# Rows of a head exchanged by copies of 32 rows on VectorE and ScalarE in place of a matrix product, and the first half of x loaded first

## What is computed

```python
def apply_rope(x, cos, sin):
    x1, x2 = jnp.split(x.astype(jnp.float32), 2, axis=-1)
    ...
    return jnp.concatenate([x1 * c - x2 * s, x2 * c + x1 * s], axis=-1).astype(x.dtype)
```

## Time and profile before

| what | value |
|---|---|
| median of 3 runs | 2049.03 us (2048.91 to 2052.25) |
| the profiled execution | 2048.79 us, its span 2047.0 us |
| TensorE | busy 1982.0 us, 97% of the span |
| VectorE | busy 1062.2 us, 52% |
| ScalarE | busy 967.0 us, 47% |
| GpSimd | busy 755.9 us, 37% |
| granted TensorE clock, mean | 0.992 of full speed |

### The profile page before, as it was taken

The page is one execution under the profiler, slowest core; times in us unless marked ns, Lnnn a source line. Parts: engine busy times, 40 slices in busy tenths (PEclk is TensorE's granted clock), DMA queues, the critical chain, the costliest instruction groups (busy, mean ns, idle before and its releaser), DMA issues.

```text
span 2047.0 us, 25966 instructions
## 1 busy us (share of the span) xinstructions
PE 1982.0 (97%) x10216; PEld 1646.8 (80%) x10216; DVE 1062.2 (52%) x1935; ACT 967.0 (47%) x1700; POOL 755.9 (37%) x341
## 2 busy tenths in 40 slices
PE   6999999999999999999999999999999999999997
PEld 6778888877778877777788888888878888888886
DVE  3365544267665667777647464312536584444214
ACT  4355534256653465555536444422555464444323
POOL 2422233433324333333343444444242324444442
PEclk9999999999999999999999999999999999999999
DMA  4311122311113222222222232333221213232332
GB/s 174 93 42 44 51 73 82 93 52 45 56 35 99 78 82 64 77 77 73 73 83 83 96 106 93 101 91 96 75 58 41 73 62 113 93 102 94 95 93 70
DMA packets 50058, 162.60 MB, mean 79 GB/s; under 512 B 5392, under 2 KB 12176, under 8 KB 49808
## 3 DMA queue, kind: packets, MB, share of 16 engines
q1 hardware_dynamic: 49504, 159.54, 24.6%
q10 hardware_dynamic: 432, 1.40, 0.2%
HBM read 158.82 MB, written 2.10 MB: 79 GB/s over the span
## 4 chain that ended last, share of the span: by engine, by line
PE 84%; DVE 11%; ACT 3%; issue 2%; DMA 0%; POOL 0%; SPq 0%; ACTq 0%; DVEq 0%
PE ps L1809 20%; PE ps L1812 20%; PE ps L1810 20%; PE ps L1859 4%; PE ps L1874 3%; PE ps L1821 2%; PE ps L1822 2%; PE ps L1824 2%; PE ps L1843 2%; PE ps L1867 2%; DVE tmp L2374 1%; DVE s_xbc L2353 1%; PE ps L1836 1%; PE ps L1834 1%; PE ps L1837 1%
## 5 line engine op out<-in xcount | busy, mean ns | idle before, releaser
L2549 POOL TENSOR_TENSOR wl<-st,wh 128x1024 fp32r<-128x1024 f32 (+2 forms) x311 | 721.8, 2323 | 1206.2 <-ACT wh L1981 1206.0
L1809 PE MATMUL ps<-xh,wh 128*128 128x512 f32 x1368 | 559.1, 409 | 0.0
L1981 ACT ACTIVATE wh<-st 128x1024 fp32r<-128x1024 f32 (+2 forms) x311 | 313.9, 1010 | 517.1 <-PE ps L1812 450.5
L1812 PE MATMUL ps<-xh,wl 128*128 128x512 f32 x1368 | 534.3, 391 | 0.0
L1810 PE MATMUL ps<-xl,wh 128*128 128x512 f32 x1368 | 533.1, 390 | 0.0
L1809 PEld LDWEIGHTS ps<-xh,wh 128*128 128x128 f32 x1368 | 257.2, 188 | 57.7 <-issue 10.9
L1812 PEld LDWEIGHTS ps<-xh,wl 128*128 128x128 f32 x1368 | 256.7, 188 | 55.8 <-POOL wl L2549 0.8
L1810 PEld LDWEIGHTS ps<-xl,wh 128*128 128x128 f32 x1368 | 257.5, 188 | 52.4 <-issue 5.3
L2508 DVE SCALAR_TENSOR_TENSOR tmp<-ps,vec,tmp 128x510 f32<-128x510 f32 (+1 forms) x176 | 131.3, 749 | 222.6 <-ACT tmp L2160 219.6
L2466 DVE SCALAR_TENSOR_TENSOR res<-res,ps 128x512 f32<-128x512 f32 (+1 forms) x37 | 22.7, 614 | 211.0 <-PE ps L1812 203.3
L1809 PE MATMUL ps<-fa_h,wh 128*128 128x512 f32 x308 | 120.6, 392 | 0.0
(11 more groups left out here) (280 smaller groups left out, 3554.1 us busy)
## 6 DMA issues: line engine op xcount, KB each, us to landing
st<-in_f_up SPq DMA_DIRECT2D x88, 512.0 KB, 3.2
st<-in_s_xbc SPq DMA_DIRECT2D x32, 512.0 KB, 3.5
st<-in_f_dn SPq DMA_DIRECT2D x32, 512.0 KB, 3.5
st<-in_o_fm SPq DMA_DIRECT2D x24, 512.0 KB, 3.5
st<-in_e_fm SPq DMA_DIRECT2D x21, 512.0 KB, 3.6
st<-in_s_z SPq DMA_DIRECT2D x16, 512.0 KB, 3.5
st<-in_s_out SPq DMA_DIRECT2D x16, 512.0 KB, 3.6
st<-in_f_dn SPq DMA_DIRECT2D x16, 384.0 KB, 3.1
```

The lines of the kernel that those rows point to most:

```text
L1809: e.matmul(u.bank.ap, hi, x.h[:, kk, :], start=first, stop=False)
L1812: e.matmul(u.bank.ap, lo, x.h[:, kk, :], start=False, stop=last).then_inc(S["mm"], 1)
L1981: e.activation(P.mem["wh"][w.m % NWR][:, 0:w.n], P.mem["stage"][w.m % NSTAGE][:, 0:w.n], ACT.Copy).then_inc(S["w_hi"], 1)
L2549: e.tensor_tensor(P.mem["wl"][w.m % NWR][:, 0:w.n], P.mem["stage"][w.m % NSTAGE][:, 0:w.n], P.mem["wh"][w.m % NWR][:, 0:w.n].bitcast(F32), ...
```

## The change

The rotation no longer uses PE: four copies, each of 32 rows and 512 columns, write g's rows in exchanged order into a tile in SBUF, each on ScalarE or on VectorE, whichever the planner's clock has free first; the product with the sine table then reads that tile. The constants are laid out anew, with the tables behind the rest, and are loaded in two parts. The first half of x no longer shares the DMA engines with the tables and the broadcast row, which come behind all of x; the second and third weights wait for the first half of x to land. The first table load of ScalarE waits for nothing. `first_norm` adds the 8 squared blocks on VectorE and sums the result with one product for each half. Small steps that need the broadcast row or the vectors are put later. The planner's times of DMAs are changed.

```diff
-    "pe": ("mm", "mm_half", "mm_tok", "ones", "blk", "perm", "score", ...
+    "pe": ("mm", "mm_half", "mm_tok", "ones", "blk", "score", ...
...
-LENGTH = {"pe": 440, "act": 620, "dve": 692, "pool": 1280, "sp": 3500, "actq": 3500}
+LENGTH = {"pe": 440, "act": 620, "dve": 692, "pool": 1280, "sp": 1300, "actq": 1300}
...
+           "y_d": 746, "gnrm": 746, "swap_a": 620, "swap_d": 390, ...
...
-PE_DEEP, HOP, OVERLAP = 165, 36, 90
+PE_DEEP, DMA_DEEP, HOP, OVERLAP = 165, 2200, 36, 90
...
-        over = [self.w[m - NSTAGE].hi, self.w[m - NSTAGE].lo] if m >= NSTAGE else []
+        over = [self.w[m - NSTAGE].hi, self.w[m - NSTAGE].lo] if m >= NSTAGE else self.xload[0] if m else []
...
     def rope_g(self, g):
         x = yield from self.taken(self.tmp)
         dst = yield from self.taken(self.tmp)
-        rp = yield from self.taken(self.aux)
-        t = yield ("perm", rp, g, g.ready)
         b2 = yield ("rope_c", dst, g, g.ready, self.rope_ready)
-        b1 = yield ("rope_s", x, rp, t, self.rope_ready)
-        rp.release(b1)
+        t = []
+        for b in range(4):
+            on = "swap_a" if self.idle["act"] + 230 < self.idle["dve"] else "swap_d"
+            rows, other = slice(32 * b, 32 * b + 32), slice(32 * (b ^ 1), 32 * (b ^ 1) + 32)
+            t.append((yield (on, x.ap[other, :], g.ap[rows, :], g.ready, x.freed)))
+        b1 = yield ("rope_s", x, t, self.rope_ready)
         b3 = yield ("rope_add", dst, x, b1, b2)
         x.release(b3)
-        g.release(t, b2)
+        g.release(b2, *t)
...
-    P.put("table", "natural_log_exp_and_others", P.pload)
+    P.put("table", "natural_log_exp_and_others", [])
...
     def first_norm(i):
         cs = HALF[i]
-        bank = yield from P.taken(P.aux)
+        ss = []
         for k in range(8):
             s = yield from P.taken(P.tmp)
-            q = yield ("sq", s.ap[:, cs], s.freed, res[:, k, cs], P.xload[i][k], 256)
-            t = yield ("ones", bank.ap[:, cs], bank.freed, s.ap[:, cs], [q, P.pload], k == 0, k == 7, 256)
-            s.release(t)
+            s.ready = [(yield ("sq", s.ap[:, cs], s.freed, res[:, k, cs], P.xload[i][k], 256))]
+            ss.append(s)
+            for s in ss[k - 2:k - 1] if k < 7 else ss[5:8]:
+                if s is not ss[0]:
+                    t = yield ("acc", ss[0].ap[:, cs], s.ap[:, cs], ss[0].ready, s.ready, 256)
+                    ss[0].ready = [t]
+                    s.release(t)
+        acc = ss[0]
+        bank = yield from P.taken(P.aux)
+        t = yield ("ones", bank.ap[:, cs], bank.freed, acc.ap[:, cs], [t, P.pload], True, True, 256)
+        acc.release(t)
...
-    P.pload = [P.put("const_in"), P.put("vec_in"), P.put("bro_in")]
+    P.pload = [P.put("const_in"), P.put("vec_in")]
...
+    P.later = [P.put("bro_in"), P.put("table_in")]
+    P.rope_ready = P.later
...
-    e.dma_start(P.mem["const"], P.T["const"]).then_inc(S["const_in"], 16)
+    e.dma_start(P.mem["const"][:, 0:C_COS], P.T["const"][:, 0:C_COS]).then_inc(S["const_in"], 16)
...
+        elif kind == "swap_a":
...
+            e.activation(dst, src, ACT.Copy).then_inc(S["swap_a"], 1)
...
+        elif kind == "swap_d":
...
+            e.tensor_copy(dst, src).then_inc(S["swap_d"], 1)
         elif kind == "rope_s":
-            x, rp, permuted, table = o
-            dve.wait_ge(permuted)
+            x, swapped, table = o
+            dve.wait_ge(swapped)
             dve.wait_ge(table)
-            dve.freed(x)
-            e.tensor_tensor(x.ap, rp.ap, P.c(C_SIN, 512), ALU.mult).then_inc(S["rope_s"], 1)
+            e.tensor_tensor(x.ap, x.ap, P.c(C_SIN, 512), ALU.mult).then_inc(S["rope_s"], 1)
...
+        elif kind == "table_in":
+            e.dma_start(mem["const"][:, C_COS:C_N], T["const"][:, C_COS:C_N]).then_inc(S["table_in"], 16)
```

More of the change, by code:

```diff
@@ L21 @@
 NWR = 3
[L23 to L32, removed]
+C_ID, C_ONE, C_BLK, C_PERM, C_TRI, C_CAUS = 0, 128, 256, 384, 512, 640
+C_INV, C_E6, C_E5, C_SGN, C_E5S, C_L20 = range(768, 774)
+C_SEL, C_COS, C_SIN = 774, 808, 1320
+C_N = 1832
 V_SIZES = [("ev_norm", 8), ("a_qn", 1), ("a_kn", 1), ("b_qn", 1), ("b_kn", 1), ("od_norm", 8),
@@ L70 @@
             "dt_e", "dt_ln", "a_exp", "ct_hi", "sel", "wend_e", "gsq", "gln", "grs", "msq", "ln_out", "ln_hi", "csq",
-            "f0", "fsilu", "sine", "lat", "q_in", "v_a", "head_hi", "gate_in", "gate_s"),
-    "dve": ("nrm", "split_lo", "v_in", "va_out", "bias_s", "bias_m", "neg_sink", "neg_g", "qk_n", "rope_s", "rope_add",
+            "f0", "fsilu", "sine", "lat", "q_in", "v_a", "head_hi", "swap_a", "gate_in", "gate_s"),
+    "dve": ("nrm", "split_lo", "v_in", "va_out", "bias_s", "bias_m", "neg_sink", "neg_g", "qk_n", "swap_d", "rope_s", "rope_add",
             "mask", "add_b", "mn", "sink_mn", "flip_d", "sink_x", "sums", "rec", "o_n", "y_g", "res_add", "acc",
@@ L78 @@
     "pool": ("w_lo", "rope_c"),
-    "sp": ("w_in0", "w_in1", "w_in2", "x_in0", "x_in1", "x_in2", "x_in3", "bias_in", "lqk_in", "pos_in", "out"),
-    "actq": ("const_in", "vec_in", "bro_in"),
+    "sp": ("w_in0", "w_in1", "w_in2", "x_in0", "x_in1", "x_in2", "x_in3", "bro_in", "table_in", "bias_in", "lqk_in",
+           "pos_in", "out"),
+    "actq": ("const_in", "vec_in"),
 }
@@ L201, in __init__ @@
         self.nsplit = self.nload = 0
-        self.idle = {n: 0.0 for n in STEPS}
+        self.idle = {n: 0.0 for n in STEPS} | {"sp": 1200.0, "actq": 700.0}
         self.ends = {}
@@ L267, in put @@
         self.idle[name] = t - (OVERLAP if name in ("act", "dve") else 0)
-        self.ends[step] = t + (PE_DEEP if name == "pe" else 0)
+        self.ends[step] = t + (PE_DEEP if name == "pe" else DMA_DEEP if kind in DMA else 0)
         return step
@@ L920, in even_layer @@
     tb, tv = [], []
-    tneg = P.put("neg_sink", P.B("sink", 0, 8), P.pload)
-    tgain = [P.put("neg_g", P.V(n), P.pload) for n in ("a_qn", "b_qn")]
+    tneg, tgain = [], []
     qs, ks = ring(mem["qz"]), ring(mem["kz"])
@@ L928, in bias @@
     def bias():
+        for n in ("a_qn", "b_qn"):
+            tgain.append((yield ("neg_g", P.V(n), P.pload)))
         for h in range(8):
@@ L931, in bias @@
             tb.append((yield ("bias_m", bt[0:64, h, 192:256], t)))
+            if h == 0:
+                tneg.append((yield ("neg_sink", P.B("sink", 0, 8), P.later)))
     def prep(fb, j, gain, rope, key, pool):
         u = yield from P.proj_g(x, [w[j]])
-        while None in gates.t[0:4]:
-            yield lambda: None not in gates.t[0:4]
+        while None in gates.t[0:4] or len(tgain) < 2:
+            yield lambda: None not in gates.t[0:4] and len(tgain) == 2
         P.start(4, P.qk_prep_g(u, (P.V(gain), tgain), rope, key, pool,
@@ L1848, in pe_program @@
             e.matmul(st.ap, P.c(C_BLK), s.ap, start=True, stop=True).then_inc(S["blk"], 1)
[L1849 to L1852, removed]
-            e.matmul(rp.ap, P.c(C_PERM), g.ap, start=True, stop=True).then_inc(S["perm"], 1)
         elif kind == "score":
@@ L2178, in act_program @@
             e.activation(hi, src, ACT.Copy, scale=scale).then_inc(S["head_hi"], 1)
+        elif kind == "swap_a":
+            dst, src, ready, freed = o
+            act.wait_ge(ready)
+            act.wait_ge(freed)
+            e.activation(dst, src, ACT.Copy).then_inc(S["swap_a"], 1)
         elif kind == "q_in":
@@ L2235, in dve_program @@
             e.scalar_tensor_tensor(dst.ap, u.bank.ap, gain, r.ap, ALU.mult, ALU.mult).then_inc(S["qk_n"], 1)
+        elif kind == "swap_d":
+            dst, src, ready, freed = o
+            dve.wait_ge(ready)
+            dve.wait_ge(freed)
+            e.tensor_copy(dst, src).then_inc(S["swap_d"], 1)
         elif kind == "rope_s":
-            x, rp, permuted, table = o
-            dve.wait_ge(permuted)
+            x, swapped, table = o
+            dve.wait_ge(swapped)
             dve.wait_ge(table)
-            dve.freed(x)
-            e.tensor_tensor(x.ap, rp.ap, P.c(C_SIN, 512), ALU.mult).then_inc(S["rope_s"], 1)
+            e.tensor_tensor(x.ap, x.ap, P.c(C_SIN, 512), ALU.mult).then_inc(S["rope_s"], 1)
         elif kind == "rope_add":
@@ L2421, in dve_program @@
             dve.wait_ge(ready)
-            dve.wait_ge(P.pload)
+            dve.wait_ge(P.later)
             dve.freed(s0)
```

16 lines of the change are left out of this document (8 added, 8 removed).

## The result

The changed kernel takes 2061.78 us (median of 4 runs, 2058.55 to 2065.17) against 2048.97 before (4 runs): a ratio of 1.006, 95% interval 1.0043 to 1.0077. It is slower by 12.8 us, where 2026 was forecast. The profiled execution took 2062.17 us with a span of 2060.4.

What follows compares the result with a forecast made beforehand. The prediction took TensorE, busy 97% of the span, as the bound; 2048.79 - 7.4 (start) - 15.4 (rotation) = 2026.0 us. Its forecast was 2018 to 2033 (54%), its wider range 2014 to 2038.

Steps and rivals of the forecast that it cites:

- Rotation: -22.4 + 7.0 = -15.4 us: All 26 rotations: 22.4 us of products leave TensorE, 7.0 come back as waits; bounds -22.4 and -5.
- the 7.0 given back: TensorE's new waits from rotations: 4.3 us for ten in the odd layer, 2.7 for the other sixteen.
- The rival that ended on this side: Slower: every copy and sine product stands behind a whole GpSimd subtraction, 9.2 us a rotation; about +27, 2076 us; 5%.
- The products' 22.4 us: Rotation: 26 products of 0.86 us each, taken off TensorE as the bound engine.
- VectorE's price: Each rotation costs VectorE 1.3 us of copies, 1.3 behind the cosine product and 0.6 of holds: 3.2 us more.
- The rule made of it: Odd layer, 450 to 600 us: VectorE's demand (136) equals TensorE's (136.3), so half of 8.6 us returns as waits, 4.3.
- Forecast -4.3 + 0.9 for the five rotations of each: Rotations outside the odd layer's two stretches: products of 0.86 us each removed, a fifth taken back as waits.
- Forecast -7.4: Start: first projection 6.9 us earlier, sums 3.0 less, a new wait of 2.5; bounds -11.9 and -4.
- One addition: 9.9: Start, first norm: after the last square at 9.4 us, one VectorE addition of 0.43 us ends at 9.9.
- the loads: Start: the two landings of x's first half come 1.8 us earlier, at 6.6 and 8.1 us.
- The new wait of 2.5 us between the halves: Start: TensorE finishes the first half at 27.5 us, the second is ready at 30; a 2.5 us wait.
- the sums' 3.0 us: Start, behind the first projection: 14 TensorE sums of 0.215 us move to VectorE, saving 3.0 us.

Runs made afterwards that it cites:

- rot_only: The kernel before with only the rotation changed to copies, its start as before: 2072.07 us, ratio 1.0099.
- no_exchange: rot_only without the copies, the sine product reading g itself, so neither product nor copies run: 2040.01 us, ratio 0.9944 to the kernel before.
- copies_beside: The kernel before, its product kept, with each rotation's four copies also run into a tile that nobody reads: 2079.65 us, ratio 1.0135.
- beside_true: copies_beside with the planner told 806 ns for a VectorE copy, 960 for sine product and add: 2064.6 us, ratio 1.0073 to the kernel before.
- start_only: The changed kernel with the old rotation by the product: 2044.94 us, ratio 0.9975 to the kernel before.
- cos_after: rot_only with GpSimd's cosine product given after the copies and waiting for them: 2066.61 us, ratio 1.0084 to the kernel before.
- rot_true: rot_only with the planner told 806 ns for a VectorE copy (was 390), 960 for sine product and add (was 692): 2038.88 us, ratio 0.9943.
- 806 and 960: Planner's ns for a VectorE copy, and for sine product and add: 2038.88 us set in rot_only, 2038.34 in the whole change.
- 700 and 850: Planner's ns for a VectorE copy, and for sine product and add: 2069.14 us set in rot_only, 2061.29 in the whole change.

## Why the prediction was wrong

**The step that failed** is "Rotation: -22.4 + 7.0 = -15.4 us", and in it the 7.0 given back. The rotation's sign was wrong: alone it costs 20 us (rot_only). The rival that ended on this side was put at 5% and made to depend on VectorE needing more than the stretch has; the stretch's work took 125 us of VectorE, less than its 150.

- *The products' 22.4 us.* In the odd layer TensorE's work fell by 11.6 us (332.3 to 320.7) for a forecast of 13.8. But no_exchange shows that only 11.5 of 22.4 come back even without copies. The rest turned into waits and clock, 7.2 us of it in the odd layer.
- *VectorE's price.* Forecast 3.2 us for a rotation; VectorE grew by 76 us, of which the 14 further sums of the start are 8, so 67/26 = 2.6. This was sized about right; the share on VectorE was 67 copies, not 78.
- *The rule made of it.* I took it that waits arise where VectorE's demand nears TensorE's, and gave back 4.3 of 8.6 us. In the odd layer they rose by 16.6 us with VectorE 64% busy. What the waits show is which step stands behind the rotation's: the copies are ready together, up to four go into VectorE's queue in a row, and the softmax's mixing and copies, for which TensorE waits with its own queue in order, stand behind them and behind whatever GpSimd holds. copies_beside shows that this costs 28 us with these planned times and beside_true 15 with others, no step waiting for the copies. A share of busy time can't show that.
- *The clock, left out.* The prediction gave the rotation's new waits no price in clock. Of the odd layer's +14.4 us the clock is +9.4: -11.6 of work, +16.6 of waits, +9.4 of clock.
- *The even layer and the latent attention.* Forecast -4.3 + 0.9 for the five rotations of each, measured +1.6 and +1.0. In the even layer TensorE's work fell by 5.1 us, but its waits went from 6.3 to 12.2 us; the clock took only 0.8 us more. In the latent attention the waits went from 7.6 to 11.6.
- *The start.* Forecast -7.4, measured -4.8 to the first full projection in the change and -7.2 in start_only. "One addition: 9.9" was mis-sized, since three sums follow the last square (10.9 in start_only), and the change's last one was held for some 2.2 us more; so the first projection gained 3.9 us and not 6.9. Of the other terms the loads came near what was worked out, the first square at 5.9 and the fifth at 8.2 us for 6.6 and 8.1, and the hold of the first xl was there. The new wait of 2.5 us between the halves did not come: from 18.72 to 41.1 us the longest wait is 0.2. Nor did the sums' 3.0 us come back in full; this stretch is 0.9 us shorter, for a forecast of 0.5. That the -7.2 of start_only is so near the forecast is in part luck, errors of both signs.
- *Holds.* Rightly foreseen that copies and the sine product would be held, up to 2.6 and 2.7 us. Not foreseen was that the copies push other instructions, down to one of a single column, behind GpSimd. cos_after shows only that a hold moved from the copies to the add gains 3 us by the ratios.

**What is settled and what is not.** Shown: the start gains, the rotation loses; the loss is TensorE's waits and the clock that falls after them, in the odd layer above all; the copies cost even where no step waits for them, and without one on VectorE 12 of the 20 us go; with the planner's times and share changed, the same rotation takes from 2039 to 2072 us. In the table the seven kernels without the product whose VectorE is busy for 227 us or more have the longest waits, 23 to 30 us; the six with 219 to 225 wait 13 to 21. But holds are counted in busy time, so this goes with the waits and is not shown to cause them. The amount of holding does not tell a good order from a bad one: summed over VectorE's instructions of the odd layer, the time above the shortest record of the same line and shape is 32 us before, 52.3 in rot_only and 51.5 in rot_true, with 26.0 and 14.5 us of waits in the last two. Of waits over 1 us for the mixing or its copy, rot_only has seven, six of them close behind a held instruction; rot_true has one. So the orders differ in what stands behind a held instruction; no run takes the holds away and keeps the order, so their share of the loss is open. Open too: why 806 and 960 give a good order and 700 and 850 a bad one. Bringing the plan to the trace helped at some values only; bringing the trace to the plan (cos_after) did not.

## What to carry to other kernels

Work taken off the bound engine comes back only where that engine does not then wait; a step moved to an engine with room is priced by who stands behind it in that engine's queue, so look up the consumers of the next three instructions, not the busy share. A wait of 2 or 3 microseconds on TensorE may cost as much again in clock, and may cost nothing: in the odd layer 16.6 us more of waits came with 9.4 of clock, in the even layer 5.9 with 0.8. Where an order is planned from a table of times, take the new step's time from a trace of the changed kernel, run neighbouring values, and trust no gain that one value alone gives; here a change of only the planned times was worth 32 us, more than the change itself.

## What the runs showed of the hardware

- The same copy of 32x512 on VectorE took 0.42 or up to 2.58 us; with its output in PSUM none of 56 took over 0.70. An operation of one column on SBUF tiles took 0.22 or, begun during GpSimd's subtraction, 2.14.
- Two starts with the same first steps differed by 2.4 us because one sum came once before and once behind GpSimd's subtraction (0.43 and 2.61 us), whose starts are 0.05 us apart (10.55 and 10.60).
- A wait of TensorE of 1.9 us cost 1.7 us more in clock; one of 2.1 us in the kernel before cost none. One of 3.0 us was followed by 5 to 6 us in which matmuls of 512 columns took 0.63 us instead of 0.40, the granted clock being at 0.63 in a window of 5 us: most of it at 1.2 GHz.
- ScalarE copies 32x512 into PSUM in 0.59 us and into SBUF in 0.63.
